# Attention on one core: inverse sums spread a step later as a product on column halves, probabilities transposed on row halves

## The reference

```python
s = einsum('bqhgd,bkhd->bhgqk', q, k) * scale      # scores, plus mask or bias (and a sink column in the window)
p = softmax(s, axis=-1)
out = einsum('bhgqk,bkhd->bqhgd', p, v)
```

## Time and profile before

| | |
|---|---|
| Median of 3 runs | 4546.93 us (4545.87 to 4550.65) |
| Profiled execution, its own time | 4549.36 us |
| Span of its instructions | 4547.6 us |
| PEld, DVE, ACT, POOL busy | 59%, 52%, 25%, 5% of the span |
| Granted TensorE clock, mean | 0.963 of full speed |
| All transpositions of probabilities, line 1841 | 1552, 225.6 us of PE |
| All value products, line 1860 | 3104 records, 206.7 us of PE |
| All scores, line 1828 | 1056 records, 289.1 us of PE |

### The profile page before, as it was taken

One profiled execution on the slowest core, in us unless ns is written; L12 is line 12 of the kernel. 1 busy time (PEld: TensorE's weight loads), 2 busy tenths in 40 slices (PEclk: granted clock), 3 DMA queues, 4 the chain that ended last, 5 costly groups with the idle time before them and its releaser, 6 DMA issues. The chain is left out here.

```text
span 4547.6 us, 66952 instructions
## 1 busy us (share of the span) xinstructions
PE 4204.4 (92%) x26760; PEld 2668.5 (59%) x26760; DVE 2375.6 (52%) x4884; ACT 1140.1 (25%) x2569; POOL 229.6 (5%) x281
## 2 busy tenths in 40 slices
PE   7997899999898999997999999989999995999997
PEld 3443756888566788664555555558757773433442
DVE  5408434433666544745555555534435546666664
ACT  2011222212564322732200000021135532110001
POOL 0100000000221000000001000000000000000000
PEclk8997999999999999997999999999999996999998
DMA  7658210222321212116666776740160014888886
GB/s 281 242 89 337 78 74 36 92 93 102 140 84 56 82 55 99 32 48 234 238 262 247 276 269 265 275 152 26 61 219 20 20 44 159 316 333 327 341 333 222
DMA packets 133315, 757.04 MB, mean 166 GB/s; under 512 B 14080, under 2 KB 52736, under 8 KB 97648
## 3 DMA queue, kind: packets, MB, share of 16 engines
q1 hardware_dynamic: 107600, 669.78, 39.1%
q0 software_dynamic: 20272, 64.76, 5.2%
q10 hardware_dynamic: 5232, 19.63, 1.2%
HBM read 663.46 MB, written 91.19 MB: 166 GB/s over the span
## 5 line engine op out<-in xcount | busy, mean ns | idle before, releaser
L440 PE MATMUL psum<-w_ring,arena 128*128 128x256 f32 (+1 forms) x2784 | 611.8, 378 | 19.3 <-PEq L199 8.3
L440 PEld LDWEIGHTS psum<-w_ring,arena 128*128 128x128 f32 x2784 | 523.6, 192 | 91.0 <-issue 20.8
L3320 PE MATMUL psum<-arena 128*64 128x512 f32 x2048 | 452.5, 594 | 0.0
L3348 PE MATMUL psum<-arena 128*128 128x512 f32 x1024 | 444.9, 592 | 0.5 <-DVE arena L3617 0.5
L440 PE MATMUL psum<-arena,w_ring 128*128 128x256 f32 x1600 | 354.9, 381 | 6.5 <-DVE arena L495 3.5
L3320 PE MATMUL psum<-w_ring,arena 128*64 128x512 f32 x1536 | 343.8, 597 | 2.3 <-issue 2.3
L440 PEld LDWEIGHTS psum<-arena,w_ring 128*128 128x128 f32 x1600 | 302.8, 191 | 50.6 <-DVE w_ring L536 3.6
L3348 PEld LDWEIGHTS psum<-arena 128*128 128x128 f32 x1024 | 192.1, 190 | 230.5 <-issue 230.5
L3320 PEld LDWEIGHTS psum<-arena 128*64 128x64 f32 x2048 | 144.9, 137 | 277.3 <-issue 277.3
L3469 ACT ACTIVATE arena<-psum 128x512 f32<-128x512 f32 x128 | 76.6, 598 | 909.2 <-PE psum L3320 909.2
L1828 PE MATMUL psum<-arena 64*128 64x256 f32 (+5 forms) x1056 | 289.1, 512 | 8.7 <-PEq L1445 3.5
(11 more groups left out here) (431 smaller groups left out, 5447.8 us busy)
## 6 DMA issues: line engine op xcount, KB each, us to landing
w_ring<-in_wstream SPq DMA_DIRECT2D x162, 2048.0 KB, 10.3
arena<-in_wstream SPq DMA_DIRECT2D x97, 2048.0 KB, 7.9
x_rows<-arena SPq DMA_DIRECT2D x26, 512.0 KB, 2.8
w_ring<-in_wstream ACTq DMA_DIRECT2D x6, 2048.0 KB, 8.5
arena<-x_rows SPq DMA_DIRECT2D x18, 512.0 KB, 7.2
xn_rows<-arena POOLq DMA_DIRECT2D x18, 512.0 KB, 7.1
arena<-f_rows SPq DMA_DIRECT2D x8, 1024.0 KB, 7.6
arena<-x_rows SPq DMA_DIRECT2D x8, 1024.0 KB, 9.2
```

Source lines behind the costliest of these rows:

```text
L440: last = self.cr.nc.tensor.matmul(out, l, r, start=(start and k == 0), stop=(k == len(pairs) - 1), skip_group_check=True)
L3320: last = nc.tensor.matmul(cr.bank[bank][HT * h:HT * (h + 1), :], left[:, k], right[:, 4 * h + k, :], start=(start and k == 0), stop=(k == ...
L3348: last = nc.tensor.matmul(cr.bank[YB[h]][:, :], hid[:, k], W[4 + h][:, k, :], start=(k == 4), stop=(k == 3))
```

## The change

It has three parts. (1) In fox and window a new `turn_halves` takes the place of `turn`: every transposition of 128 rows becomes two of 64 rows (query rows 0 to 63 into bank 4, rows 64 to 127 into bank 5, both heads side by side in each bank); it waits for both copies of the group before, and tells both banks ready only when both heads are done. The copies take a bank each, as before, and write both heads' columns of it in runs of 64. (2) The spread of step s-3 instead of s-2 is made in iteration s, in all three attentions; in fox and window by two products on column halves (`spread_halves`) in place of a transposition. `pv` is now counted up by the spread and not by the last values, and the wait for a free output bank (`ev`) moves from the spread to the first values. (3) In fox and window groups and pieces alternate (turn of group 0, scores of piece 0, turn of group 1, scores of piece 1, spread, values), and DVE's copy of group 1 stands ahead of both maxima of the second piece. In mla turns, scores and copies are as before. One further wait of ACT, for stores of an earlier stage, is added at s = 2 of fox.

```diff
     def place(eng, copy, s, g, h):
...
-        copy(t_buf[:, h, g, 0:n * P], cr.bank[4 + h][:, 0:n * P]).then_inc(te[h], 1)
+        if full_keys:
+            to, of = t_buf[:, h, g, 0:n * P], cr.bank[4 + h][:, 0:n * P]
+        else:
+            to = t_buf[:, :, g, 0:n * P].rearrange("p e (n r q) -> p e n r q", r=2, q=P // 2)[:, :, :, h]
+            of = cr.bank[4 + h].rearrange("p (e n q) -> p e n q", e=2, q=P // 2)[:, :, 0:n]
+        copy(to, of).then_inc(te[h], 1)
...
+            def turn_halves(G):
+
+                s = step_of[G]
+                g = G - goff[s]
+                n_ = len(steps[s].groups[g])
+                if G:
+                    pe.wait_ge(te[0], G)
+                    pe.wait_ge(te[1], G)
+                for h in range(2):
+                    if g == 0:
+                        pe.wait_ge(pr, 2 * s + h + 1)
+                    for n, blk in enumerate(steps[s].groups[g]):
+                        col = steps[s].pv[blk][0]
+                        for r in range(2):
+                            rows, at = slice(HD * r, HD * r + HD), 4 * HD * h + HD * n
+                            last = nc.tensor.transpose(cr.bank[4 + r][:, at:at + HD], s_buf[rows, s % 3, h, col:col + P], cr.const(C_ID)[rows, rows])
+                            if h == 1 and n == n_ - 1:
+                                last.then_inc(tr[r], 1)
+
             def spread(s):
 
-                if s % 2 == 0 and s >= 4:
-                    pe.wait_ge(ev, s // 2 - 1)
                 pe.wait_ge(inv, s + 1)
-                nc.tensor.transpose(o_bank(s)[:, 2 * P + s % 2 * P:2 * P + (s % 2 + 1) * P], rinv[:, s % 3].rearrange("p h d -> p (h d)"), cr.const(C_ID))
+                nc.tensor.transpose(o_bank(s)[:, 2 * P + s % 2 * P:2 * P + (s % 2 + 1) * P], rinv[:, s % 3].rearrange("p h d -> p (h d)"),
+                                    cr.const(C_ID)).then_inc(pv, 1)
+
+            def spread_halves(s):
+
+                pe.wait_ge(inv, s + 1)
+                for h in range(2):
+                    last = nc.tensor.matmul(o_bank(s)[h * HD:(h + 1) * HD, 2 * P + s % 2 * P:2 * P + (s % 2 + 1) * P], rinv[:, s % 3, h], cr.const(C_ID),
+                                            start=True, stop=True, skip_group_check=True)
+                last.then_inc(pv, 1)
 
             def values(G):
...
+                if g == 0 and s % 2 == 0 and s >= 4:
+                    pe.wait_ge(ev, s // 2 - 1)
...
                             pe.wait_ge(te[h], G + 1)
+                            if not full_keys:
+                                pe.wait_ge(te[1 - h], G + 1)
...
-                if g == len(s_.groups) - 1:
-                    last.then_inc(pv, 1)
-
-            for s in range(NS + 2):
+            for s in range(NS + 3):
...
-                    if ng:
-                        spread(s - 2)
+                    if s >= 3:
+                        spread(s - 3)
                 else:
-                    if ng:
-                        turn(goff[s - 2])
-                    if ng == 1:
-                        spread(s - 2)
-                    for m in range(np_):
-                        scores(s, m)
-                    if ng == 2:
-                        turn(goff[s - 2] + 1)
-                        spread(s - 2)
+                    for m in range(max(np_, ng)):
+                        if m < ng:
+                            turn_halves(goff[s - 2] + m)
+                        if m < np_:
+                            scores(s, m)
+                    if s >= 3:
+                        spread_halves(s - 3)
                 for g in range(ng):
                     values(goff[s - 2] + g)
...
+                if s == 2 and stored_by and not full_keys:
+                    cr.stored(act, stored_by)
...
                 if c == 0 and s >= 3:
                     dve.wait_ge(tr[h], goff[s - 2])
+                    if not full_keys and h == 0:
+                        dve.wait_ge(tr[1], goff[s - 2])
...
-                    if early and m == 0 and not on_act(s - 2, 1):
-                        place(dve, nc.vector.tensor_copy, s - 2, 0, 1)
+                    if early and m < old and not on_act(s - 2, 1):
+                        place(dve, nc.vector.tensor_copy, s - 2, m, 1)
...
-                    if m < old and not on_act(s - 2, 1) and not (early and m == 0):
+                    if m < old and not on_act(s - 2, 1) and not early:
                         place(dve, nc.vector.tensor_copy, s - 2, m, 1)
```

More of the change, by code:

```diff
@@ L1743, in attention @@
     qk, mx, pr, tra, trb, tea, teb, inv, pv, rc, ev, link, lt, own_ok, gated = cr.sems(
-        name, "scores maxima probs turned0 turned1 placed0 placed1 inverses products scales outputs dve late_loaded own_masks gated")
+        name, "scores maxima probs turned0 turned1 placed0 placed1 inverses finished scales outputs dve late_loaded own_masks gated")
     ld = cr.sems(name, "loaded0 loaded1")
@@ L1859, in values @@
                             pe.wait_ge(te[h], G + 1)
-                        last = nc.tensor.matmul(o[h * HD:(h + 1) * HD], s_.pv[blk][1](h), t_buf[:, h, g, n * P:(n + 1) * P],
+                            if not full_keys:
+                                pe.wait_ge(te[1 - h], G + 1)
+                        nc.tensor.matmul(o[h * HD:(h + 1) * HD], s_.pv[blk][1](h), t_buf[:, h, g, n * P:(n + 1) * P],
                                          start=(blk == 0), stop=(blk == len(s_.pv) - 1), skip_group_check=True)
-                if g == len(s_.groups) - 1:
-                    last.then_inc(pv, 1)
-            for s in range(NS + 2):
+            for s in range(NS + 3):
                 np_ = len(steps[s].pieces) if s < NS else 0
-                ng = len(steps[s - 2].groups) if s >= 2 else 0
+                ng = len(steps[s - 2].groups) if 2 <= s < NS + 2 else 0
                 if full_keys:
```

## The result

The changed kernel takes 4504.73 us (median of 4 runs, 4499.72 to 4509.33) against 4546.40 us (4 runs, 4540.15 to 4550.65): ratio 0.9905, 95% interval 0.9892 to 0.9918, 42 us faster.

A forecast was written before the change was run, and what follows sets the result against it. TensorE, busy 92%, was taken as the bound. Fox -25 us, window 0, mla 0 and tails +0.3 a call took 4549.4 to 4525; with the median 2.4 below the profiled time, 4522 (range 4500 to 4552, own case 4508 to 4538).

The forecast's parts named there:

- What bounds it: Attention: TensorE busy 92%; waits before spread 30.9 us in fox, 7.7 in window; gain from fox's blocks 3 to 5.
- Pair of halves at 0.109: Turns of fox and window: two half-row transpositions take 0.109 us, the price of a whole one; no gain, no loss.
- the layout: Priced iterations of one head pair: fox 31.45 us against 34.6, window 38.1 against 38.0.
- Shapes: Fox and window: two array shape changes a step instead of four or three, saving about 0.32 or 0.17 us.
- The wait for both copies: Second turns in fox and window wait for both heads' copies: 0.52 to 0.95 us in fox, 0.35 or 0.74 in window.
- The exponential as what is late next: Fox block 3: the turn waits 0.59 us for the second head's exponential, behind the rescaling copy; window's block 3 waits 0.3.
- Rival A: Heavy iterations of fox and window: copies end under the scores and the waits hardly show, 4488 us; chance 0.13.
- Rival B: Light iterations of fox and window win only half, as the wait only moves: about 4543 us; chance 0.17.
- rival C: Turns of fox and window: halves don't run side by side, 912 pairs cost a second pitch, 4612 us; chance 0.10.

The follow-up runs named there:

- the probe: Changed kernel plus unused transpositions on constants in its last stage, where PE is idle: a whole one 0.111 us, a pair of halves 0.065, one half 0.064.

## Why the prediction was right, and where not

**What bounds it: right.** The gain is where I looked for it: of fox's 4.55 us a head pair, 4.42 come from blocks 3 to 5 (13.93 to 9.51). The spread of the inverse sums held the scores back: the two lines moved in the run with the spread behind alone give 37.2 of the 44.5 us. mla did not move, and the stretches outside the three attentions differ by 5 us in all, though nothing in them was changed.

**Pair of halves at 0.109: the term that was mis-sized.** It is 0.065 in the probe and 0.063 in the loop (the median distance of two pairs in a turn of fox). I wrote that "below nothing it can't well go, since the same 128 stationary columns are loaded"; that bound was wrong. The Trainium skill ("TensorE: Matmul & The Clock Gate", Part 2, LDWEIGHTS) puts a load of P columns at P/1.2 ns; for 128 that makes an estimate of 107 ns. Here 32 loads of 128 stationary columns, all on one half of the rows, take 2.10 us, 0.065 each, so the measurement stands against it. The probe shows that the pitch falls to 0.065 when rows and moving columns are halved together, and that quartering them gains nothing further. Over 912 pairs 0.047 make 43 us.

The forecast missed the result by 17 us, and one pair of fox shows how much of that is this term. By start to start its turns took 6.19 where the layout had 8.92 (with the wait for the exponential in both), and all the rest 23.83 where it had 22.53: 30.02 against 31.45, which is 11 us over eight pairs. So the cheaper turns gave 22 us of fox, and the rest took 10 back. Of these 10 some 4 lie in the waits before the four second turns (5.69 with the scores ahead of them, against 5.22); the other 6 I have not taken apart. The other miss is window: 36.2 a pair (turns at 1840.14 and 1876.32) where I had 38.1, 8 us over four. The run with whole turns comes near the layout (31.1 and 37.7 a pair, turns at 1311.21 and 1342.33, 1842.64 and 1880.31), but that is luck: the layout has 3.8 us of waits a fox pair, the run has 0.4 idle before its turns and more changes of shape instead.

**Shapes: right in price** (0.15 by the probe), and of little effect.

**The wait for both copies: right in kind and near in size**, with 0.70, 0.34, 0.63, 0.78 idle in blocks 6, 7, 0, 1 where I had 0.61, 0.52, 0.77, 0.95. That it eats window's whole gain was wrong: the five-block iterations take 4.39 (blocks 5 and 7, both copies on ACT) and 3.84 (4 and 6, copies split), where the kernel before takes 3.8 to 4.3, and window became 5.9 us shorter where I had it at 154 as before.

**The exponential as what is late next: right in the changed kernel** (0.48 in block 3 against 0.59), 7.6 us in all, and by the mechanism that I gave: the rescaling copy waits for the spread, and the exponential stands behind it. What brings this is that the spread is a step later and stands behind the scores, and not the halves: with whole turns in the new order block 3 still waits 0.38 (4.2 us in 12 waits in all), with the later spread in its old place or the spread of s-2 behind the scores it hardly waits (fox: 1.0 us in one wait, and 0.2 in one).

**The rivals.** Rival A (the waits hardly show, 4488) is wrong in its mechanism, since 31.2 us of waits for copies are there; that the result lies as near to 4488 as to 4522 comes from the cheaper turns, which neither case had. Rival B (the wait only moves) was wrong in fox; rival C (halves not side by side) is refuted by the probe.

**The parts.** What I did not price apart is what each part brings alone. The later spread alone gives -43.2 in both stretches; the new order with the spread on halves (and the values' wait for both copies) adds 12.1 to that, and turns on halves take 13.4 off again: -44.5. Together these two add nothing that can be told: against the later spread alone fox is 4.7 us shorter and window 3.4 longer. That the forecast's total held owes something to luck, since it had no price below 0.109 for a pair and no term for two parts that cancel. The spread on halves was not run apart from the new order.

**Clock.** I named no such rival. It is no loss in the changed kernel (0.99 and 1.00), and perhaps a small gain: at a mean of 0.97 the lower level costs the kernel before at most 8 us of fox, at 0.99 the changed kernel at most 3 (estimates as above). Turns on halves beside the old spread do lose it in fox, from 0.97 to 0.90.

## What to carry to other kernels

Before shortening work on the engine that bounds a loop, look at which of its instructions stands in the queue ahead of work that is ready: here a 0.11 us transposition held the scores back for up to 2 us, and moving it behind them gave 37 of 45 us. When an edit has several parts, price and run each alone: here two of three cancelled. Cheaper work in front of a wait can come back as a longer wait, and with it a lower clock, as turns on halves with the old spread did (0.2% slower). In this kernel two transpositions of half the rows side by side take 0.6 of a whole one, but what reads their result then waits for both.

## What the runs showed that I had not expected

Halving a transposition, rows and moving columns together, makes it cheaper even with one half alone in the array (0.064 against 0.111), and quarters are no cheaper than halves. Idle time of 1 to 2 us before the spreads left the clock at 1.00 in most head pairs of fox in the kernel before (at 1371.36 PE had been idle for 1.99, and four 512-column records behind it take 1.13, which shows no slower pass); after its start it stood at 0.50 only twice, from 1267.9 and from 1302.0. With the cheaper turns in front of the same spread it fell in every pair, as in the 0.57 above.
